# Scale rows of the first adaLN computed row-wise on TensorE, the first pair ordered by halves of k, and the norm factor of the first FFN spread in the second pair

## The reference

```python
def modulation(cond, w, b):
    m = jax.nn.silu(cond) @ w + b
    return m.reshape(cond.shape[0], 1, N_MOD, D_MODEL)

def adaln_input(h, mod, j, g):
    return rms_norm(h, g) * (1 + mod[:, :, 3 * j + 1]) + mod[:, :, 3 * j]

def swiglu(x, w_gu, w_down):
    gate, up = jnp.split(x @ w_gu, 2, axis=-1)
    return (jax.nn.silu(gate) * up) @ w_down
```

## Time and profile before

| | us |
|---|---|
| median of 3 runs | 1561.33 (1559.12 to 1562.13) |
| the profiled execution, its own time | 1559.92 |
| its span on the core | 1558.1 |
| TensorE busy in the span | 1519.7 (98%) |
| VectorE, ScalarE, GpSimd busy | 1073.2, 616.3, 74.0 |

### The profile page before, as it was taken

The page is one execution under the profiler, slowest core; times in us unless marked ns, Lnnn a source line. Parts: engine busy times, 40 slices in busy tenths (PEclk is TensorE's granted clock), DMA queues, the critical chain, the costliest instruction groups (busy, mean ns, idle before and its releaser), DMA issues.

```text
span 1558.1 us, 23355 instructions
## 1 busy us (share of the span) xinstructions
PE 1519.7 (98%) x9159; PEld 1491.8 (96%) x9159; DVE 1073.2 (69%) x1423; ACT 616.3 (40%) x840; POOL 74.0 (5%) x59
## 2 busy tenths in 40 slices
PE   6999999989899999999999999999999999999999
PEld 6899999989759999999999999999999999999999
DVE  6886777868897866768877667797767567443323
ACT  3452332164583643322355233226643246333221
POOL 2000000023100100000020000002000010000000
PEclk9999999989999999999999999999999999999999
DMA  9345465736403244465624545563552533333332
GB/s 386 112 141 211 166 228 205 261 139 230 139 1 140 104 172 178 180 250 193 241 86 154 220 162 216 216 252 130 195 206 82 216 109 108 135 111 133 135 112 91
DMA packets 49937, 262.68 MB, mean 169 GB/s; under 512 B 6608, under 2 KB 7888, under 8 KB 27984
## 3 DMA queue, kind: packets, MB, share of 16 engines
q1 hardware_dynamic: 49872, 261.79, 45.9%
HBM read 259.54 MB, written 2.23 MB: 168 GB/s over the span
## 4 chain that ended last, share of the span: by engine, by line
PE 84%; DVE 6%; issue 4%; DMA 2%; ACT 2%; SPq 1%; POOL 0%; DVEq 0%; ACTq 0%
PE ps L1288 24%; PE ps L1290 24%; PE ps L1289 24%; PE ps L1322 3%; PE ps L1325 3%; PE ps L1323 3%; DVE mprod L827 2%; ACT w_hi L537 1%; DMA raw<-panels 1%; DMA raw_x<-panels 1%; DVE x_lo L890 1%; DVE w_lo L819 1%; DVE h L1011 1%; PE ps L1612 1%; PE ps L1516 1%
## 5 line engine op out<-in xcount | busy, mean ns | idle before, releaser
L819 DVE TENSOR_TENSOR w_lo<-raw,w_hi 128x2048 fp32r<-128x2048 f32 x163 | 373.2, 2289 | 305.0 <-ACT w_hi L537 303.6
L537 ACT ACTIVATE w_hi<-raw 128x2048 fp32r<-128x2048 f32 x164 | 314.2, 1916 | 666.7 <-PE ps L1290 506.4
L1288 PE MATMUL ps<-x_hi,w_hi 128*128 128x384 f32 (+1 forms) x1520 | 515.9, 339 | 9.8 <-DVE x_lo L890 8.6
L1289 PE MATMUL ps<-x_lo,w_hi 128*128 128x384 f32 (+1 forms) x1520 | 513.1, 338 | 0.0
L1290 PE MATMUL ps<-x_hi,w_lo 128*128 128x384 f32 (+1 forms) x1520 | 512.7, 337 | 0.0
L827 DVE SCALAR_TENSOR_TENSOR mprod<-mraw,cB 128x1024 f32<-128x1024 f32 x256 | 313.2, 1224 | 7.8
L1288 PEld LDWEIGHTS ps<-x_hi,w_hi 128*128 128x128 f32 x1520 | 286.6, 189 | 13.2 <-issue 7.4
L1289 PEld LDWEIGHTS ps<-x_lo,w_hi 128*128 128x128 f32 x1520 | 286.9, 189 | 0.7
L1290 PEld LDWEIGHTS ps<-x_hi,w_lo 128*128 128x128 f32 x1520 | 286.6, 189 | 0.0
L1290 PE MATMUL ps<-act_hi,w_lo 128*128 (+1 forms) x832 | 279.6, 336 | 0.0
L1288 PE MATMUL ps<-act_hi,w_hi 128*128 (+1 forms) x832 | 279.6, 336 | 0.0
(11 more groups left out here) (154 smaller groups left out, 1148.4 us busy)
## 6 DMA issues: line engine op xcount, KB each, us to landing
raw<-panels SPq DMA_DIRECT2D x164, 1024.0 KB, 5.2
mraw<-mod_rows SPq DMA_DIRECT2D x128, 512.0 KB, 3.5
raw_x<-panels SPq DMA_DIRECT2D x5, 1024.0 KB, 6.0
mshift<-mod_rows SPq DMA_DIRECT2D x8, 512.0 KB, 15.5
mscale<-mod_scale SPq DMA_DIRECT2D x6, 512.0 KB, 12.2
bias<-na_bias SPq DMA_DIRECT2D x4, 512.0 KB, 6.4
h<-x_in_t SPq DMA_DIRECT2D x1, 1536.0 KB, 11.0
out<-h SPq DMA_DIRECT2D x4, 384.0 KB, 2.3
```

What stands on the lines that cost most here:

```text
L537: nc.scalar.activation(w_hi[q0 % 2][:, :], raw[q0 % 2][:, :], ACT.Copy).then_inc(hi_done, 1)
L819: nc.vector.tensor_tensor(w_lo[q0 % 2][:, :], raw[q0 % 2][:, :], w_hi[q0 % 2][:, :].bitcast(F32), ALU.subtract).then_inc(lo_done, 1)
L1288: mm(out, w[0][:, cols], xs[0], start=start, stop=False)
L1289: mm(out, w[0][:, cols], xs[1], start=False, stop=False)
```

## The change

1. **Scale rows.** All eight scale tiles go to TensorE with the roles swapped: tile kk now holds 128 input features by 1024 outputs and is streamed as 2 x 512 columns past the two condition columns (`first_scale_rows`, weights 128 x 2), accumulated over kk in PSUM banks 2 and 3. ScalarE copies the two rows of 1024 into `raw[1][0:2]`, TensorE transposes them in eight small products into bank 6, VectorE makes `aT` from them in two instructions. VectorE no longer sums scale tiles 6 and 7.
2. **Loads.** cB first, then shift and scale tiles in turn; panel 0, h and the spare panel come behind scale tile 7, shift tiles 6 and 7 behind these. Panel 1 waits for the transposes (`mod_tr`), since its buffer holds the rows.
3. **Pair 0** (`first_products`): gate products of k = 0 to 3, then up products of k = 0 to 3, then gate and up by k for 4 to 7. No sums and no spreading product in it. The shift columns of `x_hi` are written by VectorE, six tiles at once.
4. **Squares and additions.** Squares come behind the splits, tiles 4 to 7 into `mscale`; VectorE does the seven additions in place of POOL.
5. **Pair 1** (`second_products`): half the gate, the sums, the other half, the spreading product, the up panel.
6. **ScalarE and VectorE in pairs 0 to 2** of the first FFN: splits are made earlier by up to one pair, scaling and shifting of `x2` later by one; `mod_sum` and `mod_out` of block 8 move from behind the split of panel 5 to the end of pair 2.

```diff
-PE_TILES = 6
-SUM_TILES = 2 * KD - PE_TILES
+SUM_TILES = KD
+EARLY_SHIFT = 6
...
-            sp.dma_start(mscale[:, 0, :], mod_scale[0]).then_inc(mscale_in[0], 16)
             sp.dma_start(cB[:, :, :], cond_rows.rearrange("(o c) k -> o c k", o=1).to_broadcast([P, 2, D])).then_inc(cb_in, 16)
...
+            for k in range(KD):
+                if k < EARLY_SHIFT:
+                    shift_tile(k)
+                scale_tile(k)
+                if k == 1:
+                    sp.dma_start(vec[:, :], vecs).then_inc(vec_in, 16)
+                elif k == 3:
+                    sp.dma_start(ident[:, :], eye).then_inc(const_in, 16)
+            panel(0, 0)
             sp.dma_start(h[:, :, :], x_in_t).then_inc(x_in, 16)
...
+            spare_panel(0)
+            for k in range(EARLY_SHIFT, KD):
+                shift_tile(k)
+            sp.wait_ge(mod_tr, 1)
             gate_up(0)
...
+            def early_pair(g):
+
+                if g == 0:
+                    split(gate_panel(0, 2), 0)
+                elif g == 2:
+                    split(gate_panel(0, 3), 0)
+                    for k in range(4, KD):
+                        shifted(0, k)
+                act.wait_ge(gs_done, g + 1)
...
+                last.then_inc(silu_done, 1)
+                if g:
+                    split(up_panel(0, g + 1), 0)
+                act.wait_ge(mul_done, g + 1)
...
+                if g == 1:
+                    for k in range(4):
+                        shifted(0, k)
...
+            for half in range(2):
+                act.wait_ge(mod_pe, KD + half)
+                nc.scalar.activation(raw[1][0:2, 512 * half:512 * half + 512], ps[0:2, 2 + half, :], ACT.Copy).then_inc(srow_done, 1)
             split(0, 0)
+            act.wait_ge(x_in, 16)
+            act.wait_ge(mvec, KD)
+            for k in range(4):
+                scaled(k)
             split_spare(0)
+            for k in range(4, KD):
+                scaled(k)
             for k in range(KD):
...
+                square_first(k)
+            split(1, 0)
+            split(2, 0)
             ffn(0)
...
+                    if b is not None:
+                        mod_sum(b, 0)
+                        mod_out(b, 0)
...
+            for k in range(EARLY_SHIFT):
                 shift_sums(k)
...
+            first_shift(slice(0, EARLY_SHIFT))
+            first_scale()
+            split(0, 0)
             for k in range(4):
+                low_first(k).then_inc(x_done, 1)
+            split_spare(0)
+            for k in range(4, EARLY_SHIFT):
+                low_first(k).then_inc(x_done, 1)
+            for k in range(EARLY_SHIFT, KD):
+                low_first(k)
+                shift_sums(k)
+                first_shift(slice(k, k + 1)).then_inc(x_done, 1)
+            split(1, 0)
+            for k in range(1, KD):
...
+                nc.vector.tensor_tensor(sqsum[:, 0:T], sq[:, 0, :] if k == 1 else sqsum[:, 0:T],
+                                        sq[:, k, :] if k < 4 else mscale[:, k, 0:T], ALU.add).then_inc(acc_done, 1)
+            split(2, 0)
...
+            def first_scale_rows():
+
+                pe.wait_ge(c_done, 1)
                 for kk in range(KD):
...
+                    pe.wait_ge(mscale_in[kk], 16)
+                    for half in range(2):
+                        last = mm(ps[0:2, 2 + half, :], cT[:, kk, :], mscale[:, kk, 512 * half:512 * half + 512],
+                                  start=(kk == 0), stop=(kk == KD - 1))
...
+                for k in range(KD):
+                    if k % 4 == 0:
+                        pe.wait_ge(srow_done, k // 4 + 1)
+                    last = nc.tensor.transpose(ps[:, 6, 2 * k:2 * k + 2], raw[1][0:2, P * k:P * k + P], ident[0:2, 0:2])
+                last.then_inc(mod_tr, 1)
...
+            def second_products():
+
+                g, u = gate_panel(0, 1), up_panel(0, 1)
+                pe.wait_ge(lo_done, g + 1)
+                feature_major(g, gate_bank(1), [(0, k) for k in range(KD)], XT)
+                norm_sums_beside(0)
+                feature_major(g, gate_bank(1), [(1, k) for k in range(KD)], XT).then_inc(pe_done, 1)
+                norm_spread(0)
...
-    scale = mod_w[0][:, D:2 * D].reshape(KD, P, KD, P).transpose(2, 1, 0, 3).reshape(KD, P, D)[:PE_TILES]
+    scale = mod_w[0][:, D:2 * D].reshape(KD, P, D)
```

More of the change, by code:

```diff
@@ L497, in norm @@
             def norm(n, last=KD):
-                for k in range(1, last):
+                for k in range(1, last if n else 0):
                     pool.wait_ge(sq_done, KD * n + k + 1)
@@ L934, in pair @@
                     if g0:
[L935 to L936 removed]
+                        if f or g0 == 2:
+                            split(gate_panel(f, g0) + 2, 0)
+                        if f == 0 and g0 == 1:
                             for k in range(4):
+                                scale_x2(k)
+                        elif f == 0:
+                            for k in range(4, KD):
                                 low_x2(k)
[L939 to L943 removed]
+                        elif g0 == 1:
+                            low_and_scale()
                         dve.wait_ge(pe_done, up_panel(f, g0) + 1)
@@ L955, in pair @@
                     last.then_inc(mul_done, 1)
-                    split(up_panel(f, g0) + 2, 0)
+                    split(gate_panel(0, 2) if f == 0 and g0 == 0 else up_panel(f, g0) + 2, 0)
                     low_act(g0, 0, done)
-                    if g0 == 0:
+                    if f == 0:
+                        if g0 == 1:
+                            low_and_scale()
+                        elif g0 == 2:
+                            dve.wait_ge(x2_done, KD)
+                    elif g0 == 0:
                         for k in range(4):
@@ L1033, in _, with shift_sums @@
             sums = [0]
-            def row_sums(rows, ready, out):
-                dve.wait_ge(ready, 16)
-                cond_sums(sums[0], 0, rows, out, mprod0)
+            def shift_sums(k):
+                dve.wait_ge(mshift_in[k], 16)
+                cond_sums(sums[0], 0, mshift[:, k, :], shsum[:, k, :], mprod0)
                 sums[0] += 1
-            def shift_sums(k):
-                row_sums(mshift[:, k, :], mshift_in[k], shsum[:, k, :])
             def first_shift(ks):
@@ L1061, in low_first, with first_scale @@
+            def first_scale():
+                dve.wait_ge(mod_tr, 1)
+                scale = ps[:, 6, 0:2 * KD].rearrange("p (k c) -> p k c", c=2)
+                link(nc.vector.tensor_tensor(aT[:, :, :], scale, mb1[:, :, None].to_broadcast([P, KD, 2]), ALU.add))
+                nc.vector.tensor_tensor(aT[:, :, :], aT[:, :, :], ngT[:, 0:KD, None].to_broadcast([P, KD, 2]), ALU.mult)                     .then_inc(mvec, KD)
             def low_first(k):
                 dve.wait_ge(xh_done, k + 1)
-                nc.vector.tensor_tensor(x_lo[:, k, T:XT], modT[:, k, :], x_hi[:, k, T:XT].bitcast(F32), ALU.subtract)
@@ L1064, in low_first @@
-                low(0, k, k)
-            def late(k):
-                row_sums(mscale[:, k, :], mscale_in[k], scsum[:, k - PE_TILES, :])
+                for cond, cols in ((0, CTX), (1, LAT)):
+                    last = nc.vector.scalar_tensor_tensor(x_lo[:, k, cols], h[:, k, cols], aT[:, k, cond:cond + 1],
+                                                          x_hi[:, k, cols].bitcast(F32), ALU.mult, ALU.subtract)
+                return last
+            for k in range(EARLY_SHIFT):
                 shift_sums(k)
-            def late_vectors(k):
-                first_shift(slice(k, k + 1))
-                first_scale(slice(k, k + 1), scsum[:, k - PE_TILES:k - PE_TILES + 1, :])
+            first_shift(slice(0, EARLY_SHIFT))
@@ L1469, in ready_ffn, with first_products, tile, gate @@
                 return waits
-            for k in range(PE_TILES):
-                mod_scale_tile(k)
-            pe.wait_ge(const_in, 16)
+            def first_products():
+                def tile(bank, w, k, a):
+                    return three(ps[:, bank + a, 0:XT], w, slice(256 * k + P * a, 256 * k + P * a + P),
+                                 (x_hi[:, k, :], x_lo[:, k, :]), k == 0, k == KD - 1)
+                def gate(k):
+                    pe.wait_ge(x_done, k + 1)
+                    return [tile(gate_bank(0), slot(0), k, a) for a in range(2)][-1]
+                def up(k):
+                    return [tile(up_bank(0), (hi_x, lo_x), k, a) for a in range(2)][-1]
+                pe.wait_ge(lo_done, 1)
+                for k in range(4):
+                    gate(k)
+                pe.wait_ge(spare_lo, 1)
+                for k in range(4):
+                    up(k)
+                for k in range(4, KD):
+                    last = gate(k)
+                    if k == KD - 1:
+                        last.then_inc(pe_done, 1)
+                    last = up(k)
+                last.then_inc(spare_pe, 1)
+            def second_products():
```

(7 more changed lines are left out.)

101 lines of the change are left out of this document (38 added, 63 removed).

## The result

The changed kernel takes **1575.72 us** (median of 4 runs, 1570.61 to 1579.18) beside 1560.22 us of the kernel before, measured with it: ratio 1.0097, 95% interval 1.0065 to 1.0128. The forecast was 1561.6 with a range up to 1566.5. The profiled execution takes 1570.61, 10.7 us more than that of before; it is the fastest of the four, so the profiles show less than the 15.5 us between the medians. No difference in this document reaches 2%; what is called slower or quicker rests on the intervals.

The account below looks back on a forecast made before the run. TensorE was taken as busy 98% of the whole, only the start offering time. Pair 4's lead shrinks from 5.5 to 0.7 us, pair 5 starts 0.3 later: +0.3 us on 1559.9, plus 1.4 to the median, 1561.6; range 1558.5 to 1566.5.

Parts of the forecast that it names:

- Row products: Scale rows on TensorE at the start: half pace for the first 5.5 us, then full pace, last ending at 26.9.
- 13 slow products in place of 17: Start of pair 0: seventeen products at 0.32 us each, as before the change, so 24 gate products take 6.7 us.
- no wait for x tiles in pair 0: Pair 0: x tiles 6 and 7 ready before needed, so the 2.44 us gap and a 1.3 one like it go.
- S: Start of the spreading product, in pair 1: forecast 61.1, 0.8 us later than the 60.31 before.
- gap of 2.55 us before pair 3: After pair 2 TensorE waits 2.2 us for VectorE's last x2_lo.
- M: Start of the first modulation sum of block 8 on VectorE: forecast 95.4, 2 us later than before.
- The gap before pair 4: TensorE, ready at 106.1, waits 4.8 us for panel 7, ready at 110.9; pair 4 starts 0.7 us earlier than before.
- The clock rival: In the gap before pair 4 the clock falls; seventeen products at 0.32 us cost 2.5 us: 1563.1 us, chance 0.20.
- Later turns average under a pair: Behind pair 5, panel turns of 17.7 or 15.6 us against 16.64 a pair: TensorE leads, the rest costs nothing.
- quick start: Rival at pair 0: first products at full pace, the spreading product at 59.5, total 1560.0 us; chance 0.12.
- slow throughout: Rival at the start: row products stay at half pace, first product at 41.5, total 1570.5 us; chance 0.14.
- Panel not held: Rival before pair 4: block 8 summed in time, TensorE keeps its lead of 5.5 us, 1555.8 us; chance 0.08.

Follow-up runs that it names:

- e1: Changed kernel with an unused 16 bytes a partition where scsum stood, so activations lie 32 bytes higher, as before: 1565.34 us, ratio 1.0013.
- e2: Kernel before with scsum allocated last, so what lay behind it moves 32 bytes down, as in the changed kernel: 1571.93 us, ratio 1.0064.
- e14: Changed kernel with 192 bytes of padding, distance 64 modulo 256 between panels and streamed tensors: 1560.54 us, ratio 0.9991.
- e3: e1 with the mraw loads queued one panel later on SP in the first FFN, so panel 7 precedes block 9's rows: 1559.59 us, ratio 0.9983.
- e4: Changed kernel with an unused tensor of 64 bytes a partition where scsum stood: 1570.46 us, ratio 1.0051.
- the sweeps: Two runs without the network, TensorE alone: 31 and 40 stretches of 96 products at chosen address offsets, the second in opposite order with nine more; no kernel time.
- e8: e3 with pair 3's first eight k waiting for x2 tiles one by one instead of for all eight: 1554.47 us, ratio 0.9954.
- e15: e8 repeated unchanged, in the session of e13: 1554.31 us, ratio 0.9952.
- e13: e8 with 96 bytes of padding in place of 32, distance 224 modulo 256: 1553.41 us, ratio 0.9940.

## Why the prediction was wrong

**Right, step by step.** Row products: half pace at first, last end at 27.2 (forecast 26.9); mod_tr 28.3 (28.4); first product 32.74 (32.6); 13 slow products in place of 17; no wait for x tiles in pair 0; S 60.85 (61.1); gap of 2.55 us before pair 3 (2.2); M 95.09 (95.4); panel 7 issued behind block 9's rows; pair 4 at 110.80 (110.9). Small errors: the last four transposes took 0.40, not 0.9. The gap before pair 4 was 4.05, not 4.8, since pair 3 started 0.2 later than forecast, took 0.2 longer at the slower pace, the panel came 0.15 earlier, and the view counts a gap from the end of the last product, not from where the next could have started. Two slips in the working cost 0.1 us each at most: the spare panel lands at 33.1 in one place and 33.4 in another, and the split of panel 7 in rows 7 ends at 109.0.

**The clock rival came true**, beside the forecast: the 4 us gap let TensorE fall to the 1.2 GHz level, with 14 products at 0.32 us behind it, 2 us (forecast 2.5 for seventeen). Shorter gaps can do the same. In e1 both gaps were followed by slow products: the 2.45 us before pair 3 by ten (90.46 to 93.34), the 2.65 us before pair 4 by ten (110.88 to 113.76), and in e2 already 1.87 us in pair 0 by ten (46.59 to 49.49). But 2.44 us in the kernel before and 2.55 us in the changed kernel were not. Of these five gaps the shortest (1.87) was followed by a fall and the second longest (2.55) was not, so the length of one gap does not decide it alone. The Trainium skill (TensorE: Matmul & The Clock Gate, "Why this matters for your kernels") asks for no long idle gaps between bursts; the trace agrees for the 4.05 us; e2 shows that even 1.87 can be long enough, and the changed kernel that 2.55 need not be.

**The step that failed** is the last of the sum: "Later turns average under a pair, so TensorE leads again and the rest of the kernel is unchanged." TensorE did lead again, and the rest was not unchanged. The change part by part listed what engines do and left out what memory does: the removal of `scsum` was costed at nothing, without a sentence. It was worth 13 us by e1 and 17 by e14, each set against the kernel before of its own session (15.5 us above it with the term, 2.2 above and 1.4 below without), and 9 to 10 us by e2, which changes nothing else; 6000 products by 2.2 ns are 13. The term can be seen by itself in the last part of the kernel, where no edit reaches. First and last start of the norm sums (30 products), before:

```profile
L1381 PE MATMUL ps<-ones,sqsum x30: 164/250/250, 55.4 to 1290.7; 128*128 128x1 f32 x30
```

after:

```profile
L1436 PE MATMUL ps<-ones,sqsum x30: 164/250/250, 56.0 to 1298.7; 128*128 128x1 f32 x30
```

From the last of them to the end of the span it is 267.4 us before, 270.1 after, 267.3 in e14 (its last at 1294.7, span 1562.0).

**Without that term** the time comes out near the forecast, in part by luck. The forecast lies 0.3 us above the kernel before; e1, which has the addresses of the kernel before, stands 2.2 above it (1565.34), e14 1.4 below (1560.54), and both medians are inside the range. Up to the down panels of the first FFN the account holds by the profiles too: the same product starts at 298.06 in the kernel before, 298.30 in e1 and 298.64 in e14 (301.80 in the changed kernel). Behind it, at the entry of the mixer, a second term shows that the sum had at nothing: by the next spreading product e1 is 5.0 us behind the kernel before and e14 5.8, and at the end of the profiles 4.9 and 3.8. In the kernel before, ScalarE's last split ahead of the squares, and the sums on TensorE that use the squares:

```profile
311.80 1.92 ACT L537 ACTIVATE w_hi<-raw 128x2048 fp32r<-128x2048 f32 x1 [5.89 <-DMA raw<-panels]
...
320.19 1.50 PE L1368 MATMUL ps<-ones,sq 128*128 128x1 f32 x12 [0.29 <-ACT sq L550]
```

and in e1:

```profile
316.93 1.92 ACT L542 ACTIVATE w_hi<-raw 128x2048 fp32r<-128x2048 f32 x1 [9.84 <-DMA raw<-panels]
...
323.90 1.50 PE L1424 MATMUL ps<-ones,sq 128*128 128x1 f32 x12 [2.31 <-ACT sq L555]
```

The panel comes 5.1 us later there, the squares stand behind its split on ScalarE, and TensorE waits for them. Of the 4.8 us that e1 loses, this wait is 2.3 and one for a split at 304.7 is 1.2; a part of the rest are sums at the 1.2 GHz level (the granted clock is 0.50 from 326 to 328). The changed kernel has no such wait, which hides a part of what its pace costs: between 298 us and that spreading product it loses 0.1 us to the kernel before, e1 4.8. So the forecast's "the rest of the kernel is unchanged" was wrong at the mixer as well, by some 5 us in these two profiles. That the medians of e1 and e14 still lie by the forecast is luck to that extent: its sum has neither this loss nor the slow products behind the gaps.

The rivals on the row products (quick start, slow throughout) are out by the timeline. "Panel not held" is out for this kernel, and e3 shows its price: 5.8 us below e1, as this rival lay 5.8 below the forecast. At 298 us e3 leads the kernel before by 5.3 us, close to this rival's 5.5; 2.9 of them are lost at the entry of the mixer, and at the end 3.3 are left.

**What stays open.** What decides between two paces at one distance (160 and 32, and 192) was not found, nor why e4's x2 went at 0.1767, a pace that distance 192 never showed in the sweeps, nor why distance 128 is 0.1755 in some kernels and 0.1760 in the sweeps. The cause inside the chip is not shown. That the period is 256 bytes, and not a multiple of it, rests on the distances 96, 64 and 32, which the sweeps reach in two ways, 256 bytes apart, with the same paces. Nor is it shown why the panel at the entry of the mixer comes late in some executions: e8 and e15 are one kernel, and from 298 us to the spreading product e8 loses 3.7 us and e15 1.0. e1 (1565.3) and e14 (1560.5) have the same pace and lie 4.8 us apart in their medians, 3.6 against the kernel before of each session, and 1.1 in their profiles; single falls of the clock, of 1.5 to 2 us each, come in one execution and not in another (from 420 to 430 us the clock is 0.83 before, in e1 and e14, and 1.00 in the changed kernel, e2, e3 and e8).

## What to carry to other kernels

When a change adds or drops a buffer, compare addresses before timing: everything allocated behind it moves, and a product stream may change its pace by up to 2% (0.1733 to 0.1767 us here) with no wait to show for it. In a profile that reads as a fully busy engine with fewer instructions per stretch; put the bytes back, or take them from the old kernel, before looking for a cause in the schedule. Set each run against the old kernel of its own session, and follow one product through two profiles: the term at the mixer shows in no median. And when an engine is made to come earlier, look at the queue order behind it: the gain (7 us here, from e14's 1560.5 to e13's 1553.4) lay in one load order and one wait that had been harmless before.

## What the runs showed of the hardware

- The step of a dense 384-column fp32r product is 0.1733 us at best and up to 0.1767 (0.1778 with an offset of 8 bytes), depending on where weights and streamed tensor lie in SBUF; what sorts the paces in these runs is their distance modulo 256 bytes. Distances 96 and 128 were slow in all 21 stretches and five kernels, 224, 0 and 64 quick in all 12 stretches and two kernels. The Trainium skill (Advanced Engine Details and Errata, "SBUF Cachelines") speaks of 16-byte lines and says that hits on one line run at full performance. All offsets here but one (8 bytes, 0.1775 and 0.1778) are multiples of 16, so by that rule alone they would change nothing; the runs show that they do.
- At some distances two paces exist, and a stretch keeps the one that it enters with: offset 32 gave 0.1734, 0.1767 and 0.1734 again in one execution, 50 us apart.
- Two weights-to-stream distances mixed (x_hi at offset 32, x_lo at 0, or the reverse) gave 0.1744, between the two.
- TensorE's granted clock fell to the 1.2 GHz level behind gaps of 1.87 us (e2), 2.45 and 2.65 us (e1), 4.05 us (changed kernel) and 4.37 us (e14), with 10 to 14 products at 0.32 us each time, and stayed at the 2.4 GHz level behind 2.44 us (before) and 2.55 us (changed kernel). In e1, e2 and e14 the first products behind the gap still start 0.17 to 0.18 us apart, and only then 0.32.
